# Output stage of a hybrid decoder step: both products in split fp32r passes, low parts on VectorE and GpSimd

## What is computed

```python
h = rmsnorm(x, norm1_g) * (1 + sc1) + sh1
z = h @ w_in                                    # split into three groups of heads
oa, ob, oc = hgrn2(z), rg_lru(z), delta_net(z)  # oa, oc: gated_head_norm
mo = concatenate([oa, ob, oc], -1) @ w_out      # (288, 1024) @ (1024, 1024)
x = x + gt1 * mo
h = rmsnorm(x, norm2_g) * (1 + sc2) + sh2
q = h @ peer_wq                                 # (288, 1024) @ (1024, 1024)
x = x + gt2 * experts(h, q)                     # top-k product keys, 16384 experts
```

```python
def gated_head_norm(o, z, g):
    y = o * rsqrt(mean(o * o, -1) + EPS)        # mean over the 64 columns of a head
    return y * g * silu(z)
```

## Time and profile before

| | us |
|---|---|
| median of 3 executions | 2402.75 |
| lowest and highest | 2393.02 and 2404.12 |
| the profiled execution | 2402.28 |
| its span, first to last instruction | 2400.5 |
| TensorE busy, share of the span | 2280.2, 95% |
| VectorE, ScalarE, GpSimd busy | 1524.4, 1232.4, 1094.2 |
| mean granted clock of TensorE | 0.965 of 2.4 GHz |

### The profile page before, as it was taken

The page is one execution under the profiler, slowest core; times in us unless marked ns, Lnnn a source line. Parts: engine busy times, 40 slices in busy tenths (PEclk is TensorE's granted clock), DMA queues, the critical chain, the costliest instruction groups (busy, mean ns, idle before and its releaser), DMA issues. The chain is left out here.

```text
span 2400.5 us, 58522 instructions
## 1 busy us (share of the span) xinstructions
PE 2280.2 (95%) x20492; PEld 2093.1 (87%) x20514; DVE 1524.4 (64%) x3131; ACT 1232.4 (51%) x2351; POOL 1094.2 (46%) x1000
## 2 busy tenths in 40 slices
PE   6978999999999999999989799999999999999998
PEld 4954868999998799999979367799999978999997
DVE  2747635973225968888657575289532278787885
ACT  2540214567556955555536212165675588555554
POOL 0005105884446746566300330088744475565661
PEclk8988999999999999999989789999999999999999
DMA  6566034556552079899544740455555512898993
GB/s 262 165 242 236 3 115 159 176 183 202 190 185 97 10 262 312 275 309 309 177 147 163 287 144 11 142 173 178 197 188 186 189 45 74 284 316 276 311 309 102
DMA packets 123821, 455.53 MB, mean 190 GB/s; under 512 B 13744, under 2 KB 14256, under 8 KB 122544
## 3 DMA queue, kind: packets, MB, share of 16 engines
q1 hardware_dynamic: 105264, 386.80, 45.8%
q0 software_dynamic: 18432, 67.12, 10.2%
HBM read 449.37 MB, written 4.49 MB: 189 GB/s over the span
## 5 line engine op out<-in xcount | busy, mean ns | idle before, releaser
L415 POOL TENSOR_TENSOR parts<-ring,parts 128x512 fp32r<-128x512 f32 x358 | 463.5, 1297 | 473.8 <-ACT parts L408 459.4
L408 ACT ACTIVATE parts<-ring 128x512 fp32r<-128x512 f32 x616 | 386.5, 632 | 360.3 <-PE ps_u L464 281.3
L2582 PE MATMUL ps_y<-act_parts,parts 128*128 128x256 f32 x4096 | 565.5, 280 | 0.0
L460 PE MATMUL ps_u<-h_parts,parts 128*128 128x256 f32 x4096 | 563.5, 280 | 0.9 <-ACT parts L408 0.6
L2582 PEld LDWEIGHTS ps_y<-act_parts,parts 128*128 128x128 f32 x4096 | 518.8, 189 | 0.9 <-issue 0.3
L460 PEld LDWEIGHTS ps_u<-h_parts,parts 128*128 128x128 f32 x4096 | 514.3, 188 | 3.3 <-ACT parts L408 1.9
L415 DVE TENSOR_TENSOR parts<-ring,parts 128x512 fp32r<-128x512 f32 x258 | 177.6, 691 | 382.5 <-ACT parts L408 359.7
L2631 POOL TENSOR_TENSOR act_parts<-big,act_parts 128x256 fp32r<-128x256 f32 x256 | 245.3, 958 | 310.5 <-ACT act_parts L2611 310.5
L464 PE MATMUL ps_u<-h_parts,parts 128*128 128x256 f32 x2048 | 322.5, 279 | 1.4 <-DVE parts L415 1.1
L2586 PE MATMUL ps_y<-act_parts,parts 128*128 128x256 f32 x2048 | 323.6, 280 | 0.0
L2586 PEld LDWEIGHTS ps_y<-act_parts,parts 128*128 128x128 f32 x2048 | 277.0, 188 | 0.0
(11 more groups left out here) (391 smaller groups left out, 2874.0 us busy)
## 6 DMA issues: line engine op xcount, KB each, us to landing
ring<-in_stream SPq DMA_DIRECT2D x522, 512.0 KB, 4.1
more_ring<-in_stream SPq DMA_DIRECT2D x126, 512.0 KB, 5.1
extra_ring<-in_stream SPq DMA_DIRECT2D x48, 512.0 KB, 5.7
big<-in_stream SPq DMA_DIRECT2D x16, 512.0 KB, 11.7
out_state_out<-big SPq DMA_DIRECT2D x2, 1440.0 KB, 9.1
big<-in_state SPq DMA_DIRECT2D x2, 1280.0 KB, 10.6
big<-in_mixc SPq DMA_DIRECT2D x2, 1024.0 KB, 7.9
big<-in_spots SPq DMA_DIRECT2D x2, 1024.0 KB, 5.5
```

Of the source, the lines that this page charges most:

```text
L408: eng.activation(m.parts[:, q % PARTS, 0, :], half_tile(m, t, half), ACT.Copy).then_inc(s["hi_ready"], 1)
L415: eng.tensor_tensor(m.parts[:, q % PARTS, 1, :], half_tile(m, t, half), m.parts[:, q % PARTS, 0, :].bitcast(F32), ALU.subtract).then_inc(m ...
L460: pe.matmul(out, hi[:, k, :], hr[:, side, kk, 0:tokens], start=(kk + side == 0), stop=False)
L2582: pe.matmul(ps[:, half * KD // 2 + k, :], hi[:, k, :], act_parts[:, j % AHEAD, side, :], start=False, stop=False)
```

## The change

`output_block` multiplies as the other blocks do. Every half tile q (0 to 15 of `w_out`, 16 to 31 of `peer_wq`) is split into `m.parts`: high by ScalarE, low by VectorE for q under 8 and by GpSimd from 8 on. The activations are split too, with all 288 columns: `m.mixed` for the first product (`mixed_high`, `mixed_low`), h for the second (`column_high`, `column_low`). The tensor `h_parts` grows from 256 to 288 columns and is packed by k, and after a wide column of h has been used, its place takes the 256-column pair that the experts read (`narrow`, `again_high`). The gates are multiplied in before the spreads. A ring slot is given back by the low part of a tile's second half. A step with `w_out` or `peer_wq` is now `product`: eight matmuls with the high part, four with the low. The query product goes by half tiles, too, heads 0 to 3 and then 4 to 7 of each k, and the copies of the query are shared between ScalarE (heads 0, 1, 4, 6) and VectorE (2, 3, 5, 7).

```diff
@@ ScalarE
+            def high(q):
+                t, w = weights(q)
+                if q % 2 == 0:
+                    m.wait_tile(act, t)
+                if q >= PARTS:
+                    act.wait_ge(s["parts_used"], q - PARTS + 1)
+                act.activation(m.parts[:, q % PARTS, 0, :], w, ACT.Copy).then_inc(s["hi_ready"], 1)
...
+            high(0)
+            mixed_high(0)
+            act.activation(tmp[:, 0, 0:1], m.eps, ACT.Sqrt).then_inc(s["root_loaded"], 1)
             act.wait_ge(s["sums_ready"], 1)
             act.activation(norm, ps[0:12, 4, 0:NT], ACT.Sqrt, bias=m.eps[0:12, :], scale=1.0 / HD).then_inc(s["root_ready"], 1)
...
+            for i in range(1, READY):
+                mixed_high(i)
+                high(i)
+            for i in range(READY, KD):
+                act.wait_ge(s["normed"], i - READY + 1)
+                mixed_high(i)
+                high(i)
+            for q in range(KD, KD + PARTS):
+                high(q)
+            squares(0, HALF)
+            for q in range(KD + PARTS, OUT_Q + 2):
+                high(q)
+            squares(HALF, KD)
             act.wait_ge(s["sums2"], 1)
             root_of_mean(act, m, ps[:, 0, 0:NT]).then_inc(s["root2"], 1)
...
+            column_high(0)
+            column_high(1)
+            high(OUT_Q + 2)
+            column_high(2)
+            for k in range(3, KD):
+                column_high(k)
+                high(OUT_Q + k)
+            def again_high(k):
+                act.wait_ge(s["parts_used"], OUT_Q + 2 * k + 2)
+                act.activation(narrow[:, 0, k, :], m.h[:, k, 0:NP], ACT.Copy).then_inc(s["u_hi"], 1)
+
+            again_high(0)
+            again_high(1)
+            for q in range(OUT_Q + KD, ALL_Q):
+                high(q)
+                if q % 2:
+                    again_high((q - OUT_Q - 5) // 2)
+            again_high(KD - 2)
+            again_high(KD - 1)
+            for h in COPY_ACT:
+                wait_head(act, h)
                 act.activation(m.query[:, h, :], ps[:, h, 0:NT], ACT.Copy).then_inc(s["query_out"], 1)
@@ GpSimd
+            for q in range(KD, ALL_Q):
+                t, w = weights(q)
+                pool.wait_ge(s["hi_ready"], q + 1)
+                pool.tensor_tensor(m.parts[:, q % PARTS, 1, :], w, m.parts[:, q % PARTS, 0, :].bitcast(F32),
+                                   ALU.subtract).then_inc(m.done[t % RING] if q % 2 else s["late_low"], 1)
@@ VectorE
+            mixed_low(0)
+            low(0)
+            v.wait_ge(s["squares_ready"], 2)
+            for n, t in enumerate(tiles[:2]):
+                v.tensor_tensor(m.mixed[:, t, :], m.mixed[:, t, :], m.zact[:, 6 + t, :], ALU.mult).then_inc(s["gated"], 1)
             v.wait_ge(s["root_ready"], 1)
             v.reciprocal(norm, norm).then_inc(s["inverse"], 1)
...
+            v.tensor_tensor(m.mixed[:, 5:8, :], m.mixed[:, 5:8, :], m.zact[:, 11:14, :], ALU.mult).then_inc(s["gated"], 1)
+            for i in range(1, READY):
+                mixed_low(i)
+                low(i)
...
                 if n:
-                    gated(n - 1)
-            gated(len(tiles) - 1)
+                    mixed_low(READY + n - 1)
+                    low(READY + n - 1)
+            mixed_low(KD - 1)
+            low(KD - 1)
...
             for k in scale_shift(steps, m, 1, s["h_ready"]):
-                pass
...
+                if k:
+                    column_low(k - 1)
+            column_low(KD - 1)
             for k in range(KD):
...
+                v.wait_ge(s["u_hi"], k + 1)
+                v.tensor_tensor(narrow[:, 1, k, :], m.h[:, k, 0:NP], narrow[:, 0, k, :].bitcast(F32), ALU.subtract).then_inc(
+                    s["u_lo"], 1)
+            for h in COPY_DVE:
+                wait_head(v, h)
+                v.tensor_copy(m.query[:, h, :], ps[:, h, 0:NT])
@@ TensorE
+            def product(q, first, k, begin, end, ready):
+
+                hi, lo = m.parts[:, q % PARTS, 0, :], m.parts[:, q % PARTS, 1, :]
+                pe.wait_ge(s["hi_ready"], q + 1)
+                for n in range(HALF):
+                    for side in range(2):
+                        pe.matmul(ps[:, first + n, 0:NT], hi[:, n * P:(n + 1) * P], hr[:, side, k, :],
+                                  start=begin and side == 0, stop=False)
...
+                for n in range(HALF):
+                    mm = pe.matmul(ps[:, first + n, 0:NT], lo[:, n * P:(n + 1) * P], hr[:, 0, k, :], start=False, stop=end)
...
+            def out_product(half, first, end):
                 for i in range(first, end):
...
+                    pe.wait_ge(s["mix_lo"], i + 1)
+                    product(half * KD + i, half * HALF, OUT_K[i], i == 0, i == KD - 1, s["out_ready"])
...
             for k in range(KD):
...
+                pe.wait_ge(s["h_lo"], k + 1)
+                for half in range(2):
+                    product(OUT_Q + 2 * k + half, half * HALF, k, k == 0, k == KD - 1, s["query_ready"])
```

More of the change, by code:

```diff
@@ L2013, in _, with column_high, squares @@
+            def column_high(k):
+                act.wait_ge(s["h_ready"], 2 * k + 2)
+                act.activation(hr[:, 0, k, :], m.h[:, k, :], ACT.Copy).then_inc(s["h_hi"], 1)
+            def squares(first, end):
+                for k in range(first, end):
+                    act.wait_ge(s["x_ready"], 2 * k + 2)
+                    square_column(act, m, k, s["squares2"])
             act.activation(sq[:, 0:2, :], m.mixed[:, 0:2, :], ACT.Square).then_inc(s["squares_ready"], 1)
             act.activation(sq[:, 2:5, :], m.mixed[:, 5:8, :], ACT.Square).then_inc(s["squares_ready"], 1)
+            high(0)
@@ L2045, in _ @@
+            for i in range(1, READY):
+                mixed_low(i)
+                low(i)
+            v.wait_ge(s["gated"], 3)
             for n, t in enumerate(tiles):
@@ L2073, in _ @@
+            for h in COPY_DVE:
+                wait_head(v, h)
+                v.tensor_copy(m.query[:, h, :], ps[:, h, 0:NT])
+            v.wait_ge(s["u_lo"], KD)
         @block.tensor
         def _(pe):
-            def half_product(half, first, end):
-                for i in range(first, end):
[L2078 to L2081, removed]
-                    if k in tiles:
-                        pe.wait_ge(s["normed"], tiles.index(k) + 1)
-                    for n in range(HALF):
-                        mm = pe.matmul(ps[:, half * HALF + n, 0:NT], w[:, n * P:(n + 1) * P], m.mixed[:, k, :],
-                                       start=(i == 0), stop=(i == KD - 1))
-                        if i == KD - 1 and n < HALF - 1:
-                            mm.then_inc(s["out_ready"], 1)
-                    if i % 2:
-                        mm.then_inc(m.done[t % RING], 1)
+            def product(q, first, k, begin, end, ready):
[5 more added lines that the diff above has]
+                                  start=begin and side == 0, stop=False)
+                t, _ = weights(q)
+                if q % 2:
+                    m.wait_done(pe, t)
+                else:
+                    pe.wait_ge(s["lo_ready" if q < KD else "late_low"], (q if q < KD else q - KD) // 2 + 1)
+                for n in range(HALF):
+                    mm = pe.matmul(ps[:, first + n, 0:NT], lo[:, n * P:(n + 1) * P], hr[:, 0, k, :], start=False, stop=end)
+                    if end and n < HALF - 1:
+                        mm.then_inc(ready, 1)
+                mm.then_inc(s["parts_used"], 1)
@@ L2737, in build @@
             delta_block(nc, m, l)
-            with nc.sbuf_tensor("h_parts", [P, 2, KD, NP], F32R) as hr:
-                output_block(nc, m, l, hr, stream, small_out, state_out)
-                experts_block(nc, m, l, hr, stream, spots_in)
+            with nc.sbuf_tensor("h_parts", [P, KD * 2 * NT], F32R) as parts:
+                wide = parts.rearrange("p (k s t) -> p s k t", s=2, t=NT)
+                narrow = parts[:, 0:KD * 2 * NP].rearrange("p (k s t) -> p s k t", s=2, t=NP)
+                output_block(nc, m, l, wide, narrow, stream, small_out, state_out)
+                experts_block(nc, m, l, narrow, stream, spots_in)
             gates_block(nc, m, l)
```

79 lines of the change are left out of this document (37 added, 42 removed).

## The result

| | before | changed |
|---|---|---|
| median, us | 2401.83 | 2410.25 |
| lowest to highest, us (8 executions each) | 2393.02 to 2410.49 | 2405.52 to 2418.65 |
| span of the profiled execution, us | 2400.5 | 2408.4 |
| mean granted clock | 0.965 | 0.954 |

What follows compares the result with a forecast made beforehand. TensorE was taken as the bound, busy 2280.2 of 2400.5 us. From 2402.3 us, 7.6 saved over two layers and 4.3 added for half clock gave 2399.0 us, range 2387 to 2410.

Steps and rivals of the forecast that it cites:

- the one on the clock: Half clock after TensorE idling: 1.7 us before scores in both layers, 0.9 at layer 0's start; 4.3 us together.
- new wait of 2.7 us: Output product's start, layer 0: TensorE waits 2.7 us for VectorE's second low column before the second half tile.
- second half: Second half of the output product: eight half tiles and four column sums take 14.7 us; 2.55 us won.
- query: Query product: 25.5 us where it took 31.1, both longer by 1.9 us for the half clock there.
- tail: After the query product: last narrow column and copies give back 2.1 us; TensorE idles 3.5 us before the scores.
- Half tile every 1.593 us: Both products: a split half tile takes 1.593 us instead of 1.944, saving 22.5 us over both layers.
- Residual, root, query start: Between the products: root only 1.5 us sooner, 1.25 us given back at the first column, query starts 0.25 us sooner.
- three-quarters rival: Both products: three passes take three quarters of four's time, 1.458 us a half tile; 2386 us, chance 0.05.
- A wait for a part: Between half tiles: TensorE waiting for a weight tile or a part would show the prediction wrong; no size given.
- The clock-holds rival: At the two new gaps the granted clock does not fall; 2394.7 us, chance 0.22.
- everything arrives: Seams hidden better than worked out, so all 22.5 us saved in the products arrives; 2380 us, chance 0.08.
- The rival of VectorE against GpSimd: Query columns: both engines serialise, costing 11.7 us, deciding from 3.19 us a column; 2411 us, chance 0.12.

Runs made afterwards that it cites:

- the filled wait: Changed kernel with eleven bf16 matmuls on constants filling TensorE's wait before the second half tile; 2401.73 us, ratio 0.9991 to the kernel before.
- the three half tiles: Changed kernel with the third half tile's product ahead of the four spreads instead of behind them; 2401.90 us, ratio 1.0003 to the kernel before.
- the wait in the kernel before: Kernel before, f32 products, with an extra VectorE reciprocal for which TensorE's second step of the output product waits; 2412.38 us, ratio 1.0040.
- the first experiment: Changed kernel with the split of the second half tile and its column moved ahead of root and gatings; 2395.20 us, ratio 0.9965 to the kernel before.
- the mended versions: Changed kernel with second split and early copies moved ahead and norm wait and tail filled, without or with six low parts moved to VectorE; 2386.81 and 2384.20 us.
- the last experiment: Changed kernel with all seams mended plus six more low parts on VectorE (half tiles 18 to 23); 2384.20 us, ratio 0.9925 to the kernel before.
- the move of six low parts: Low parts of half tiles 18 to 23 made on VectorE; alone in the changed kernel 2405.33 us, with all seams mended 2384.20 us.
- the filled norm: Changed kernel with 24 bf16 matmuls on constants after the last column sum, where TensorE waits for the norm; 2411.87 us, ratio 1.0035 to the kernel before.
- that kernel: Changed kernel with only the output product split in fp32r passes, the query product f32 as before; 2409.81 us, ratio 1.0026 to the kernel before.
- all seams mended: Changed kernel with second half tile's split and early copies moved ahead, norm wait filled, seven matmuls after the first copy; 2386.81 us, ratio 0.9944.

## Why the prediction was wrong

**The step that failed is the one on the clock.** The sum had 4.3 us for it, with bounds 0 and 12; it cost 13.2: 10.1 at the two starts, worked out next, and 1.5 a layer over the scores. The prediction gave the start of layer 0 "even odds 1.7 us: 0.9" and the start of layer 1 nothing more than it had. The new wait of 2.7 us was foreseen, measured 2.65 on the weight loads and 2.41 on the matmuls. Its consequence was not: 13.6 us at half clock in both layers. The first residual comes at 28.0 and not 22.1 in layer 0, and at 28.0 and not 23.8 (22.5 + 1.3) in layer 1: 5.9 + 4.2 = 10.1 us in the place of 0.9. The other terms, below, were off by about +0.2 (second half), +0.8 (query) and -0.3 us (tail) a layer. 2399.0 - 0.9 + 10.1 + 2 x 0.7 = 2409.6; the profiled run took 2410.26. That the two meet so closely is in part luck, since the stretches outside the stage differ by +3.3, -3.9 and +1.0 us between the two profiles. I had priced a fall by its shortest length, from the earlier trace rows, and had not asked what brings the clock back: behind the wait stand one half tile, four spreads of 12 rows, one half tile and a fifth spread, and half tiles in a row only after that. The experiments with the filled wait, with the three half tiles and with the wait in the kernel before show the chain: behind the wait the clock falls in nine of ten stages, and it stays down while the spreads and single half tiles follow. Whether it is the 12 rows of the spreads which keep it down, or the short gaps around them, was not separated.

**Half tile every 1.593 us:** right in all full-clock stretches (326.18 to 327.78 above; the pace of the earlier trace rows). The three-quarters rival (1.458) is refuted. Second half 14.9 us from first to fifth residual, predicted 14.7.

**Residual, root, query start:** 3.8 us from fifth residual to root, 5.4 from root to query, both as worked out.

**Query:** 28.2 us, predicted 27.4; its weight loads wait 0.33 and 0.27 us there, for a high part of ScalarE and a low part of GpSimd. The term was 0.8 too small. A wait for a part was also what the prediction named as a sign of being wrong; it came, but small.

**Tail:** idle time of 3.13 us before the scores (predicted 3.5), and the fall behind it in both layers, 3.61 us of scores instead of 2.06, predicted 1.7 a layer.

**The clock-holds rival**, 2394.7, was not met: the clock fell at both new gaps, in both layers. That the first experiment measures 2395.20 is chance. There the new wait is gone too (2.2 us a layer), and the fall over the scores stays (1.5 us a layer). The 2380 of **everything arrives** isn't reached by the mended versions either, 2387 and 2384. **The rival of VectorE against GpSimd** I had marked down, from 0.15 us in the earlier trace rows. The changed kernel's timeline has scale and shift instructions of 0.41 us that take 1.38 beside a GpSimd subtraction, which itself takes 1.80 instead of 1.29:

```profile
355.51 1.80 POOL L2097 TENSOR_TENSOR parts<-ring,parts 128x512 fp32r<-128x512 f32 x1 [9.52 <-ACT parts L2033]
...
356.09 1.38 DVE L352 TENSOR_SCALAR big<-big,gain,mod 128x256 f32<-128x256 f32 x1
...
359.01 3.66 POOL L2097 TENSOR_TENSOR parts<-ring,parts 128x512 fp32r<-128x512 f32 x2 [1.70 <-ACT parts L2033]
...
359.49 1.32 DVE L351 TENSOR_TENSOR big<-big,gain 128x32 f32<-128x32 f32 x1
```

The scale and shift takes over three times as long as alone, and the 32 columns of gain, 0.19 us alone, 1.32. So the engines hold each other up far more than the 0.15 us said. With GpSimd idle over these columns, in the last experiment, both are back at 0.41 and 0.19. The full block which the Trainium skill states (SBUF — State Buffer, Who interferes with whom) fits these rows better than mine did. The rival's own marks were not reached, though: GpSimd's low parts average 1.41 us (1.45 was the mark), and VectorE's columns come on average 1.9 us apart, 3.5 at most, where 3.19 each was to decide. So it has a cost, but not the 11.7 us of full serialising. The cost was small because the half clock lay over the same microseconds: 0.7 to 0.8 us in a layer of the changed kernel, 2.5 us once the clock holds (30.8 against 28.3), by what the move of six low parts gave back. The two stalls lie over each other: the filled norm, which removes the half clock alone, gave nothing.

**Could it have been seen?** The row of layer 1 showed a fall at this very place with no wait right before it, and the earlier trace rows one after 1.79 us. Both said that the place stood at the edge. A new wait of 2.7 us there deserved odds near one. And the fall deserved a length with two ends, from the 3.4 us of the shortest one to the return of dense work. In my own schedule the wait ended at 307.0 and the fourth half tile, from which on nothing comes between, started at 313.7: 6.7 us at full clock, up to twice that at half clock. That is an estimate, made afterwards, of 3 to 13 us at half clock, 2 to 7 us a layer; 13.6 and 6.2 were measured.

## What to carry to other kernels

Price a new wait of TensorE twice: the wait, and the half clock until full-array work runs again without gaps. Here a wait of 2.41 us cost 2.2 us itself and up to 6.2 us more. Look at what stands right behind the wait. Where weak matmuls (few rows, waits between them) follow, put dense products before them, or fill the wait with matmuls that nobody reads. And try the removal of overlapping stalls together, since one can hide the other's price.

## What the runs showed of the hardware

The same instructions with the same wait of 2.41 us met no fall in layer 0 and 10.3 us of half clock in layer 1 of one execution. So the length of the gap alone does not decide. The 12 executions of that kernel spread over 19 us, the slower ones at a lower mean granted clock. The Trainium skill (TensorE: Matmul & The Clock Gate, What's actually happening) says that the gate's monitor runs freely and is not tied to the program's start; these two layers are consistent with that and don't prove it.

bf16 matmuls of 512 columns on constants kept the clock up: 24 of them over 5.3 us left 1.00 in the stretch that was at 0.51. Eleven of them, over 2.55 us, left none of the half clock right behind the wait, but 3.4 us of it some 4 us later.

A VectorE instruction with one SBUF tensor input (the scale and shift of 256 columns, 0.41 us) was held up beside GpSimd as well: 1.38 us, and 1.51 in the version with all seams mended.
